# Splitting the gate marking of a PEER layer between GpSimd, ScalarE and VectorE

## The reference, cut to what matters

```
v1, i1 = lax.top_k(s1, 16)            # 128 first keys
v2, i2 = lax.top_k(s2, 16)            # 128 second keys
cand = v1[..., :, None] + v2[..., None, :]      # 256 candidates
top_s, pos = lax.top_k(cand, 16)
eidx = i1*128 + i2 of those;  gates = softmax(top_s)
act = gelu(u_tab[eidx] . x) * gates
y   = act @ v_tab[eidx]
```

## Time and profile before

| what | value |
|---|---|
| median of three runs | 4005.1 us |
| the profiled execution | 4007.24 us, span 4005.5 us |
| TensorE busy | 3726.1 us (93%) |
| VectorE busy | 2876.5 us (72%) |
| ScalarE busy | 1145.2 us (29%) |
| GpSimd busy | 1077.0 us (27%) |
| the changed stage | 1830.14 us (first mark) to 1962.53 us (end of the last keep), 132.4 us |

### The profile page before, as it was taken

One profiled execution on the slowest core, in us unless ns is written; L12 is line 12 of the kernel. 1 busy time (PEld: TensorE's weight loads), 2 busy tenths in 40 slices (PEclk: granted clock), 3 DMA queues, 4 the chain that ended last, 5 costly groups with the idle time before them and its releaser, 6 DMA issues.

```text
span 4005.5 us, 59549 instructions
## 1 busy us (share of the span) xinstructions
PE 3726.1 (93%) x21032; PEld 3308.2 (83%) x21032; DVE 2876.5 (72%) x4130; ACT 1145.2 (29%) x1790; POOL 1077.0 (27%) x922
## 2 busy tenths in 40 slices
PE   7999999999995987976799999999999999999998
PEld 3688778778774863445699999999999999999997
DVE  2564665665565333999688888888888888888898
ACT  1212222222222212117623233233322323223231
POOL 1343444344430624011021221212212122121220
PEclk9999999999996988998999999999999999999999
DMA  9443333333334423123588888888888888888895
GB/s 362 150 123 114 107 113 118 112 112 121 115 105 152 159 74 106 72 73 137 217 312 308 327 308 300 317 321 321 307 309 321 310 322 313 301 322 309 324 338 223
DMA packets 338730, 887.11 MB, mean 221 GB/s; under 512 B 114098, under 2 KB 116594, under 8 KB 274674
## 3 DMA queue, kind: packets, MB, share of 16 engines
q1 hardware_dynamic: 290290, 546.63, 40.0%
q0 software_dynamic: 46080, 335.56, 22.3%
q10 hardware_dynamic: 2304, 4.20, 0.3%
HBM read 849.54 MB, written 35.69 MB: 221 GB/s over the span
## 4 chain that ended last, share of the span: by engine, by line
PE 40%; DMA 5%; DVE 3%; ACT 1%; DVEq 1%; issue 0%; SPq 0%; ACTq 0%
PE PS L1834 7%; PE PS L1833 7%; PE PS L1835 7%; PE PS L1223 7%; PE PS L1225 6%; PE PS L1224 6%; DMA UR<-peer_ut 5%; DVE UL L1209 1%; ACT UH L1205 1%; DMA VR<-peer_v 1%; DVEq L1966 1%; DVE Ub L1964 0%; PE PS L1862 0%; PE PS L1857 0%; DVEq L1951 0%
## 5 line engine op out<-in xcount | busy, mean ns | idle before, releaser
L1223 PE MATMUL PS<-xh,UH 128*128 128x352 f32 x2048 | 664.6, 325 | 27.4 <-POOL UL L1209 17.6
L1834 PE MATMUL PS<-AL,VH 128*128 128x352 f32 x2048 | 668.8, 327 | 0.0
L1225 PE MATMUL PS<-xh,UL 128*128 128x352 f32 x2048 | 663.0, 324 | 0.0
L1224 PE MATMUL PS<-xl,UH 128*128 128x352 f32 x2048 | 658.7, 322 | 0.0
L373 PE MATMUL PS<-hH,WH 128*128 128x512 f32 (+1 forms) x1312 | 483.6, 369 | 8.4 <-ACT kk L688 7.4
L374 PE MATMUL PS<-hL,WH 128*128 128x512 f32 (+1 forms) x1312 | 463.7, 353 | 0.0
L375 PE MATMUL PS<-hH,WL 128*128 128x512 f32 (+1 forms) x1312 | 462.9, 353 | 0.0
L1786 POOL DMA_INDIRECT Ub<-peer_u,stage x160 | 203.2, 1270 | 935.3 <-DVE Ub L1964 897.9
L1223 PEld LDWEIGHTS PS<-xh,UH 128*128 128x128 f32 x2048 | 385.0, 188 | 34.5 <-issue 17.8
L1224 PEld LDWEIGHTS PS<-xl,UH 128*128 128x128 f32 x2048 | 388.3, 190 | 0.0
L1834 PEld LDWEIGHTS PS<-AL,VH 128*128 128x128 f32 x2048 | 385.9, 188 | 0.0
(11 more groups left out here) (330 smaller groups left out, 7012.9 us busy)
## 6 DMA issues: line engine op xcount, KB each, us to landing
UR<-peer_ut SPq DMA_DIRECT2D x128, 1024.0 KB, 7.2
VR<-peer_v SPq DMA_DIRECT2D x256, 512.0 KB, 6.2
AW<-wada SPq DMA_DIRECT2D x128, 512.0 KB, 3.9
WR<-wseq SPq DMA_DIRECT2D x224, 256.0 KB, 2.6
wr<-wada SPq DMA_DIRECT2D x32, 1024.0 KB, 11.1
gates_dram<-GS SPq DMA_DIRECT2D x11, 2048.0 KB, 6.3
GB<-gates_dram SPq DMA_DIRECT2D x64, 352.0 KB, 8.6
oR<-wout SPq DMA_DIRECT2D x32, 512.0 KB, 3.8
```

What stands on the lines that cost most here:

```text
L1223: pe.matmul(dst, UH[:, j % 2, k, :], xh[:, k, :], start=(k == 0), stop=False)
L1224: pe.matmul(dst, UH[:, j % 2, k, :], xl[:, k, :], start=False, stop=False)
L1225: last = pe.matmul(dst, UL[:, j % 2, k, :], xh[:, k, :], start=False, stop=(k == KT - 1))
L1834: pe.matmul(low, VH[:, slot, j, cols], AL[:, :, b, :], start=False, stop=False)
```

## The change

`GACT` goes from 6 to 4, and a new `GPOOL` = 3 is added. Of the eight W1 tokens of a unit GpSimd now makes tokens 0 to 2 by a tensor_scalar each (compare and weigh), VectorE token 3 in that way, and tokens 4 to 7 are compared by VectorE in one tensor_tensor and weighed by ScalarE. O2 stays whole on VectorE. GpSimd waits for the same semaphore as VectorE (the matmuls of the unit four before), and TensorE waits for one more semaphore, `s_wp`. GpSimd's instructions of the 44 units are written out, and `u_low` of block (1, 0) comes behind them.

```
-GACT = 6
+GPOOL = 3
+GACT = 4
...
+        s_wp = sem("keys_marked_and_weighted_pool")
...
                             pe.wait_ge(s_wa1, 8 * r + j + 1)
+                            pe.wait_ge(s_wp, 8 * r + j + 1)
...
-                    for j in range(SUPER + 1):
-                        u_low(pool, j // SUPER, j % SUPER)
+                    for j in range(SUPER):
+                        u_low(pool, 0, j)
+                    pool.wait_ge(s_prev, 1)
+                    pool.sem_inc(s_passed)
+                    for n in range(GUNITS):
+                        pool.wait_ge(s_gpe, n + 1)
+                        pool.sem_inc(s_passed)
+                        for t in range(GU * n, GU * n + GPOOL):
+                            last = pool.tensor_scalar(W1[:, n % GSLOTS, t % GU, :], iota, pairT[:, 0, t:t + 1], pairT[:, 2, t:t + 1],
+                                                      ALU.is_equal, ALU.mult)
+                        last.then_inc(s_wp, 1)
+                    u_low(pool, 1, 0)
...
-                            for i in range(GU - GACT):
+                            for i in range(GPOOL, GU - GACT):
```

## The result

The changed kernel took 4042.97 us (median of four, 4041.41 to 4049.96) against 4003.65 us for the kernel before (four runs, 4001.86 to 4010.14): a ratio of 1.0099, 95% interval 1.0081 to 1.0116. The forecast was 3992, with a range up to 4012.

The account below looks back on a forecast made before the run. ScalarE was taken to bound the stage at 2.66 us a unit, VectorE afterwards at 2.5. 14.4 us gained less 1.5 gave 12.9: from 4007.24 to 3994.3, with the median 2.1 lower 3992; range 3984 to 4012.

Parts of the forecast that it names:

- The bound before, and that the stage's end passes on to the program's end: Stage before: ScalarE bounds at 2.66 us a unit; whatever the stage's end moves, the program's end moves by the same.
- ScalarE's part: ScalarE's loop in the stage: two activations fewer take 0.59 us off 2.66, leaving 2.07 us a unit.
- GpSimd's instruction at 0.35 us, at most 0.45: GpSimd's new tensor_scalar, priced between affine select (0.287 us) and two-input tensor_tensor (0.45); three make about 1.05 us a unit.
- Who pays for the lock: VectorE beside GpSimd: each GpSimd instruction of duration d costs VectorE d - 0.19, so 3 x 0.16 us a unit.
- the rule of the earlier trace: From tensor_tensors of both engines: they take turns, one whole instruction each; VectorE loses the other's duration less some 0.19 us.
- GpSimd itself is last: Rival: each GpSimd instruction waits behind one of VectorE's, up to 1.07 us; pace stays 2.5 to 2.8; no own chance.
- p: VectorE's predicted time a unit in the changed stage, GpSimd's hold included: taken as 2.5 us; break-even at 2.9.
- Both signs of being wrong: In the changed profile: VectorE's L1680 instruction staying at 1.23 us, or TensorE's units over 2.9 us apart.
- The Trainium skill's rule: Port shared by GpSimd and VectorE: exclusive lock held for the whole instruction, loser fully blocked; treated as second rival, 0.20.
- The second rival: Whole-instruction lock or longer GpSimd instruction: p = 3.14, 4013 us; with 0.45 us p = 3.6, 4028; chance 0.20.
- The sum by slots and stretches: TensorE followed through 44 units, four slots and two dense blocks: stage end 14.4 us earlier; 1856.4 + 36 p if VectorE bounds.
- 1.5 us for the moved `u_low`: Block (1, 0)'s 4.5 us GpSimd instruction, now behind the units, may block VectorE's last marks: 1.5 us lost (0 to 3).

Follow-up runs that it names:

- e10: The changed kernel itself, unaltered, measured again in a second series: 4040.82 us, ratio 1.0083 against the kernel before.
- e1: The changed kernel with VectorE's two tensor_tensors of a unit reading iota from PSUM instead of SBUF: 3993.3 us, ratio 0.9965 against the kernel before.
- e5: The changed kernel with iota in PSUM for VectorE and tokens split GpSimd 2, ScalarE 4, VectorE 2: 3990.5 us, ratio 0.9953 against the kernel before.
- e8: e4 with one VectorE tensor_scalar moved between its two two-input instructions: 3992.24 us, ratio 0.9960 against the kernel before.
- e4: The changed kernel with tokens split GpSimd 2, ScalarE 4, VectorE 2, iota in SBUF: 4013.83 us, ratio 1.0011 against the kernel before.
- e6: The changed kernel with a VectorE drain behind each of its two two-input instructions, iota in SBUF: 4032.72 us, ratio 1.0062 against the kernel before.
- e11: The same kernel as e5, measured again with more rounds: 3991.55 us, ratio 0.9959 against the kernel before.
- e7: e1 with GpSimd's second token not weighed and its third made with immediate scalars only; executed once, 3989.57 us, only instruction durations read.
- e9: e1 with GpSimd's work replaced by compare alone, plain copy, and 256-element compare and multiply with immediates; executed once, 3985.43 us, only durations read.
- e2: Control: the kernel before with iota in PSUM for VectorE and nothing on GpSimd: 4012.15 us, ratio 1.0004 against the kernel before.

## Why the prediction was wrong, step by step

- **The bound before, and that the stage's end passes on to the program's end.** Right: a reload 31.7 us later gave 33 us (e10), one 18.9 us earlier gave 17 us (e1).
- **ScalarE's part,** 2.07 us a unit with four tokens. Right: where GpSimd isn't in the way, ScalarE bounds the stretches behind the dense blocks at 2.08 us (e1, e5, e8), and units 16 to 31 of e5 took 30.14 us from start to start for the 30.2 of the sum. **VectorE's own 2.00 us.** Right: 1831.51 to 1833.50 in e1 (1.99), 2.05 in the changed kernel.
- **GpSimd's instruction at 0.35 us, at most 0.45.** Wrong by more than two: 0.787. This is the first failed step. I took the affine select and the two-input tensor_tensor for its neighbours because the names and the number of inputs were near; the one costs 0.29 us, as a plain copy does, and a compare with a multiply costs 3.4 ns an element and 0.07 for each scalar fetched. By itself this would have done no harm: 3 x 0.78 = 2.34 us a unit is still under 2.66, and e1, with just this price and no lock, ran 17 us faster than before, near the 12.9 forecast.
- **Who pays for the lock.** Wrong, and this is what turned the sign. The step was "one GpSimd instruction of duration d costs VectorE d - 0.19", three times a unit, and nothing for GpSimd. Measured: VectorE lost 0.05 us a unit, and GpSimd, kept out through both of VectorE's two-input instructions, lost 1.27. e1 (no second SBUF input: nothing lost), e4 (about the same loss once a unit, with two tokens) and e8 (a second opening: 0.92 us a unit, and two instructions beside each of VectorE's units) show it. The rows had half of it: in the earlier trace rows GpSimd's two instructions of 4.5 us took 10.75 together, 1.7 lost, and the sum carried no such term.
- **Why the rule of the earlier trace rows did not carry over.** Not because VectorE pauses there (its code drains between the instructions): in e6 it pauses too and pays next to nothing, and in e5 it does not pause and a tensor_scalar of it pays 4.0 us to a `u_low`, where the changed kernel's pay 0.06. What differs is GpSimd's instruction. One of 4.5 us with two inputs held VectorE up to its end, one of 0.79 us with one input only for some 0.27 us (the estimate in e8). Whether the length or the kind makes the difference no run here separates.
- **"GpSimd itself is last" with no chance of its own.** I named the mechanism, that VectorE gets ahead, is stopped by its slots and leaves room, and then let it keep "the same 2.5 to 2.8". With 0.787 and 1.27 in it, that sum is 3.6. "Slower" had a chance of 0.20, but for another mechanism, a VectorE held up by whole instructions; that its case with 0.45 us also has p = 3.6 is a coincidence (and its 4028 leaves out the 1.5 us; with them it is 4030). Both signs of being wrong came at once: L1680's instruction did not get longer, and units were over 2.9 us apart.
- **The Trainium skill's rule** ("SBUF — State Buffer", "Who interferes with whom": the port pair is an exclusive lock and the later one fully blocks). Its direction was right and I gave it 0.20. The second rival used it for VectorE's time, where it does not hold for the new instruction: in e8 one of 0.79 us delays VectorE by 0.09, and to its end would be 0.6 more than the opening of 0.18. For GpSimd behind VectorE it holds to the full, over two instructions in a row, and for VectorE behind `u_low` too (e5, 4.34 us for 0.33).
- **The sum by slots and stretches.** Its form was right. With 3.6 for p, 1856.4 + 36 p gives 1986.0 for the last keep's end; measured 1994.1. Of these 8.1 us 2.9 arose in the first stretch (VectorE and GpSimd start together, and TensorE began only at 1835.8), 4.1 in the second and 0.8 in the third, where VectorE fills several slots in a row and GpSimd gets one instruction done in each 2.05 us, and 0.3 in the dense blocks and at the end.
- **1.5 us for the moved `u_low`.** Nothing in the changed kernel: it ran from 1990.72 for 4.51 us, after VectorE's last mark, and inside the time of the last store. The reasoning was right all the same: in e5 and e11, where GpSimd is done earlier, it held VectorE up for 4.0 us ("up to 4.3" was forecast), and that cost 0.7 us.

## What to carry to other kernels

Before giving GpSimd a share, look at what VectorE runs beside it: two-input instructions from SBUF without a pause kept GpSimd out for nearly their whole length, however short its own were, so put a tensor_scalar between them or one input in PSUM. Price a GpSimd instruction by one with the same operations over the elements, not by the nearest name. When a contention is read from a trace, write down what each of the two engines lost, and carry the numbers over only to instructions of the same kind and length: here a GpSimd tensor_tensor of 4.5 us made VectorE pay, a tensor_scalar of 0.79 us made GpSimd pay.

## What the runs showed of the hardware that was not expected

- A GpSimd tensor_scalar with compare and multiply on 128 x 128 float32 takes 0.79 us with two scalars from SBUF, 0.71 with one, 0.64 with none; compare alone 0.60 with one; a copy 0.29; 256 elements without scalars from SBUF 1.07 us (e7, e9).
- VectorE's tensor_scalar with two scalars from SBUF does not keep GpSimd out as the two-input instructions do: it is the place at which GpSimd got in (e8, 0.96 to 1.60 us for GpSimd's instruction instead of 2.05). It can be held up itself: 4.34 us instead of 0.33 beside a GpSimd tensor_tensor of 4.5 us (e5, e11).
- A GpSimd tensor_scalar of 0.79 us holds up VectorE's next two-input instruction by 0.09 us, when that begins 0.18 us behind the last one (e8).
- A tensor_tensor of VectorE is as fast with one input in PSUM (1.208 us for 1024 elements, e2) as with both in SBUF (1.21 to 1.23).
